# Seven half-size products for the query, key, value and gate projections of two state-space layers, and modulation sums and the rotation's swap moved off VectorE

## The reference

```python
for l in range(2):
    shift, scale, gate = split(silu(c) @ w_ada[l] + b_ada[l], 3)          # 2048 -> 3 x 2048
    h = rms_norm(x, norm_g[l]) * (1 + scale) + shift
    u, z_s, q, k, v, z_a = split(h @ w_in[l])                             # six of 1024 columns
    y_s = s5_mixer(u, ...) * silu(z_s)      # complex diagonal scan, GELU, 1024 -> 2048 GLU
    q, k = rope(q), rope(k)                 # 8 heads, two maps of 64 in each
    w = softmax(q0 k0) - lam * softmax(q1 k1)                             # causal
    y_a = rms_norm(w @ v, sub_g) * (1 - lambda_init) * silu(z_a)
    x = x + gate * (concat(y_s, y_a) @ w_out[l])                          # 2048 -> 2048
x = rms_norm(x, final_g)
x = x + gate * ((sigmoid(ga) * delta(h2) + sigmoid(gb) * window(h2)) @ w_out_2)
```

## Time and profile before

| | |
|---|---|
| Median of 3 runs | 4215.18 us (4211.24 to 4215.89) |
| Profiled execution | 4209.86 us, span of its instructions 4208.0 us |
| PE busy | 4067.2 us, 97% |
| DVE busy | 2275.8 us, 54% |
| ACT busy | 811.7 us, 19% |
| POOL busy | 496.1 us, 12% |
| Mean granted TensorE clock | 0.986 |
| HBM | 118 GB/s over the span |

### The profile page before, as it was taken

The page is one execution under the profiler, slowest core; times in us unless marked ns, Lnnn a source line. Parts: engine busy times, 40 slices in busy tenths (PEclk is TensorE's granted clock), DMA queues, the critical chain, the costliest instruction groups (busy, mean ns, idle before and its releaser), DMA issues.

```text
span 4208.0 us, 40928 instructions
## 1 busy us (share of the span) xinstructions
PE 4067.2 (97%) x15864; PEld 2733.2 (65%) x15864; DVE 2275.8 (54%) x4174; ACT 811.7 (19%) x1483; POOL 496.1 (12%) x808
## 2 busy tenths in 40 slices
PE   6999999999999999999999989999999999999999
PEld 3665544444446655444458758888888888888888
DVE  6666536664533665365656535454555347666643
ACT  2232201132012222011321222222222122320000
POOL 0233111111111332111111000000000011100000
PEclk8999999999999999999999999999999999999999
DMA  9533332334552333323345342121212243424423
GB/s 335 191 122 106 108 127 96 129 110 153 150 165 90 117 107 109 127 96 127 111 146 165 100 129 71 61 76 61 75 61 76 80 131 123 143 91 150 130 95 105
DMA packets 370127, 499.27 MB, mean 119 GB/s; under 512 B 44315, under 2 KB 279182, under 8 KB 369422
## 3 DMA queue, kind: packets, MB, share of 16 engines
q1 hardware_dynamic: 290048, 340.16, 24.9%
q0 software_dynamic: 38480, 125.86, 9.7%
q10 hardware_dynamic: 41406, 30.63, 2.3%
HBM read 462.51 MB, written 34.08 MB: 118 GB/s over the span
## 4 chain that ended last, share of the span: by engine, by line
PE 87%; DVE 8%; ACT 2%; DMA 1%; issue 1%; ACTq 0%; POOL 0%; DVEq 0%; SPq 0%; POOLq 0%
PE bank L108 85%; PE bank L111 2%; DVE tring L123 2%; DVE tring L129 2%; ACT tring L116 1%; DMA side<-in_w_ada 1%; DVE wring L123 1%; DVE dring L123 0%; DVE bank L123 0%; DVE tring L126 0%; DVE region_a L123 0%; DVE dring L126 0%; ACT L116 0%; DVE region_b L123 0%; DVE s_delta L123 0%
## 5 line engine op out<-in xcount | busy, mean ns | idle before, releaser
L108 PE MATMUL bank<-region_b,wring 128*128 128x256 f32 (+1 forms) x4416 | 1309.0, 450 | 5.0 <-ACT region_b L116 3.9
L108 PEld LDWEIGHTS bank<-region_b,wring 128*128 128x128 f32 x4416 | 829.1, 191 | 397.1 <-issue 315.8
L108 PE MATMUL bank<-region_a,wring 128*128 128x256 f32 (+1 forms) x3232 | 1067.7, 483 | 1.7 <-DVE wring L123 1.7
L108 PEld LDWEIGHTS bank<-region_a,wring 128*128 128x128 f32 x3232 | 604.7, 191 | 381.6 <-issue 335.7
L153 POOL DMA_DIRECT2D side<-in_w_ada x384 | 209.0, 545 | 1294.4 <-DVE tring L129 927.8
L129 DVE SCALAR_TENSOR_TENSOR tring<-side,cact,tring 128x512 f32<-128x512 f32 x360 | 303.0, 842 | 74.2 <-DMA side<-in_w_ada 38.4
L123 DVE TENSOR_TENSOR tring<-bank,tring 128x256 f32<-128x256 f32 (+1 forms) x229 | 101.1, 442 | 334.0 <-PE bank L108 331.0
L108 PE MATMUL bank<-wring,region_b 128*128 128x512 f32 (+1 forms) x640 | 267.5, 574 | 7.2 <-ACT region_b L116 7.2
L123 DVE TENSOR_TENSOR wring<-wring 128x1024 f32<-128x1024 f32 (+1 forms) x213 | 234.8, 1103 | 24.2 <-PE bank L108 15.2
L108 PE MATMUL bank<-wring,region_a 128*128 128x512 f32 x512 | 226.5, 600 | 4.4 <-ACT region_a L116 4.4
L108 PEld LDWEIGHTS bank<-wring,region_b 128*128 128x128 f32 x640 | 152.2, 241 | 118.2 <-issue 87.0
(11 more groups left out here) (288 smaller groups left out, 4261.5 us busy)
## 6 DMA issues: line engine op xcount, KB each, us to landing
wring<-in_w_in SPq DMA_DIRECT2D x178, 1024.0 KB, 5.3
side<-in_w_ada POOLq DMA_DIRECT2D x384, 256.0 KB, 3.1
wring<-in_w_out SPq DMA_DIRECT2D x48, 1024.0 KB, 8.0
yaT<-in_w_ada SPq DMA_DIRECT2D x16, 1024.0 KB, 9.2
wring<-in_w_glu SPq DMA_DIRECT2D x16, 1024.0 KB, 7.4
tring<-x_saved SPq DMA_DIRECT2D x48, 256.0 KB, 3.1
gring<-in_w_ada POOLq DMA_DIRECT2D x43, 256.0 KB, 3.0
SS<-in_w_ada SPq DMA_DIRECT2D x8, 1024.0 KB, 9.2
```

Of the source, the lines that this page charges most:

```text
L108: return self.e.matmul(*a, **k) if self.e else self
```

## The change

- `za`, `zs`, `q`, `k`, `v` of both layers and the first layer's output projection become seven-product jobs. `open_split` makes the quarter sums of `h`: one of them in place over `h`'s own quarter, two in `yaT`, one in `region`'s u tiles, so the last two wait for the `u` fence. The value jobs are `turned`: the weights stream in 128 columns against activations as stationary operand, 16 instead of 8 matmuls for each of the seven.
- `za` is stored in DRAM like `zs` (`save_z`) and fetched for each head in attention (`za_fetch`, SP's queue) into new places (`ya_tile`).
- Modulation sums: ACT scales the row in place, POOL adds it (`ada_sum` on both). DVE has no part in it.
- Rotation: ACT copies the four 32-partition pieces swapped from PSUM, DVE multiplies the whole tile by a sine table with changed signs.
- The next layer's parameters are cut in smaller steps, taken at 0.6 instead of 0.2 a step; the first output powers and angles move behind the next layer's norm; new tiles wait for the `out` fence.
- In the second block the quarter sums move from before the values product into its second half, and the band's rows are made earlier.
- Interleaving rates: 65 and 69 of 79 for 73 and 77, 40/37 for 45/37, opening 1.5 for 1.6.

```diff
@@ beside_states
-            yield from dense(u_job(l, 512))
+            open_split(l)
+            for n, _ in enumerate(dense(u_job(l, 512))):
+                if n == 12:
+                    for k in range(0, HT, 4):
+                        quarter(h_split[l], k, 4)
+                yield
             for h0 in range(0, HT, 2):
-                for n, _ in enumerate(dense(layer_dense(l, d["w_in"][l], 5 * HALF + h0 * P, "keep_za", h0))):
-                    if h0 == 0 and n == 3:
+                for n, _ in enumerate(gate_products(l, h0, "za", 5 * HALF)):
+                    if h0 == 0 and n == 1:
                         turn_u(l, 512)
+                        do("pe_fence", "u", l)
+                        for name in ("quarter_rest", "quarter_last"):
+                            for k in range(0, HT, 4):
+                                do(name, h_split[l], k, 4)
                     yield
...
+        def split_job(l, n0, use, *args, s3, turned_=False):
+            parts = h_split[l]
+            return Dense(d["w_in"][l], KT, n0, 256, False, None, parts.ready, use, (l, *args), parts, s3, None, turned_)
+        def gate_products(l, h0, name, n0):
+            yield from fast(split_job(l, n0 + h0 * P, "save_z", h0, name, s3=states_s3[l]),
+                            before=lambda j: temps.take(name, l, h0 + j), done=lambda j: temps.give(name, l, h0 + j))
@@ value_products
-            yield from dense(layer_dense(l, d["w_in"][l], 4 * HALF + h0 * P, "keep_v", h0, tokens="blocks", n=512))
+            for h in (h0, h0 + 2):
+                yield from fast(split_job(l, 4 * HALF + h * P, "keep_v", h, s3=lay[l]["s3_in"], turned_=True))
@@ block_one
-            interleave(state_space(l), beside, [73, 77][l] / 79)
+            do("pe_fence", "first_u", l)
+            interleave(state_space(l), beside, [65, 69][l] / 79)
-            interleave(attention(l), beside_attention(l), 45 / 37, 32, 1.6)
+            interleave(attention(l), beside_attention(l), 40 / 37, 32, 1.5)
...
-                interleave(add_gated(l, d["w_out"][l], lambda k: xT[:, k, :] if k < HT else yaT[:, k - HT, :], ready),
-                           state_space_params(1), 0.2)
+                interleave(gated, state_space_params(1), 0.6)
@@ tensor: seventh
+                        if job.turned:
+                            i = pe.matmul(bank[:, n * P:n * P + P], moving[:, n * P:n * P + P], weights[:, k, :], start=k == 0, stop=k == half - 1)
@@ vector: ada_sum removed; scalar:
+            def ada_sum(m, n0, k):
+                w = ada_slots(m).at("ada", m, n0, k)[:, 0, :]
+                act.wait_ge(*ada_landed(m, n0, k).of("ada", m, n0, k))
+                if k == 0:
+                    room(temps.clear("acc", m, n0))
+                act.activation(w if k else temps.at("acc", m, n0), w, ACT.Copy, scale=cact[:, mods[m][0] // 2, k:k + 1]).then_inc(
+                    *rows_scaled.up(m, n0, k))
@@ gpsimd
+            def ada_sum(m, n0, k):
+                if k == 0:
+                    return
+                acc = temps.at("acc", m, n0)
+                pool.wait_ge(*rows_scaled.of(m, n0, k))
+                own()
+                pool.tensor_tensor(acc, acc, ada_slots(m).at("ada", m, n0, k)[:, 0, :], AD).then_inc(*rows_added.up(m, n0, k))
+                ada_slots(m).leave(("ada", m, n0, k), pool.mine())
@@ scalar: rotate
+                for s in range(4):
+                    a, z = 32 * s, 32 * (s ^ 1)
+                    act.activation(y[z:z + 32, :], bank[a:a + 32, :], ACT.Copy).then_inc(
+                        *(att_a.up("swapped", l, h0, which, j) if s == 3 else a_step.up()))
@@ sync
+            def za_fetch(l, h):
+                sp.wait_ge(*stored("za", l, h).of("za", l, h))
+                room(passed("ssm", l) if h < HT // 2 else [valued.of(l, 3)])
+                sp.dma_start(ya_tile(l, h), za_saved[l, h]).then_inc(*za_in[h].landing(l))
@@ second block
-        for k in range(0, HT, 4):
-            quarter(h_parts, k, 4)
-            do("quarter_rest", h_parts, k, 4)
...
-        run_all(dense(vb_job))
+        values_ = dense(vb_job)
+        for n in range(6):
+            next(values_)
+        temps.take("band")
+        do("band_rows")
+        for k in range(0, HT, 4):
+            quarter(h_parts, k, 4)
+            for n in range(2):
+                next(values_)
+            do("quarter_rest", h_parts, k, 4)
+        run_all(values_)
...
+        products = gdn_products(0, 2)
+        for n in range(2):
+            next(products)
         aux.take("band")
```

More of the change, by code:

```diff
@@ L220 @@
     more: Any = None
+    turned: bool = False
     @property
@@ L494, in build, with fast @@
         jobs = []
-        def fast(job, after=None, late=()):
+        def fast(job, after=None, late=(), before=None, done=None):
             jid = len(jobs)
@@ L847, in state_space_params, with params @@
             temps.give("prow", l)
-            for part in range(2):
[L849 to L853, removed]
-                do("ssm_fetch", l, 2 + part)
[L855 to L859, removed]
+            def params(part, stages=1):
+                for stage in range(stages):
+                    do("ssm_params", l, part, stage)
+                    if l:
+                        yield
+                if not l:
+                    yield
+            for part in range(2):
+                yield from params(2 * part, 1 if part else 5)
+                yield from params(2 * part + 1, 1 if part else 5)
+                do("ssm_fetch", l, 2 + part)
+            yield from params(4, 4)
             for i in range(4):
@@ L947, in beside_attention @@
             yield from glu(l)
-        def dense_rotated(job, l, h0, which):
-            g = dense(job)
-            for j in range(2):
-                for name in ("rx", "ry"):
-                    temps.take(name, l, h0, which, j)
-            for _ in g:
-                yield
-            for j in range(2):
-                for name in ("rx", "ry"):
-                    temps.give(name, l, h0, which, j)
         def attention(l):
@@ L1498, in seventh @@
                     pe.wait_ge(*folded.of(jid, 0))
-                for k in range(half):
-                    if part < 4:
-                        room(parts.ready(half * (part // 2) + k))
-                        moving = parts.quarter(part, k)
-                    else:
-                        pe.wait_ge(*quarters_summed.of(parts.name, part - 4, parts.chunk[k]))
-                        moving = parts.sums[part - 4][:, k, :]
-                    i = pe.matmul(bank, weights[:, k, :], moving, start=k == 0, stop=k == half - 1)
+                for n in range(2 if job.turned else 1):
+                    for k in range(half):
+                        if part < 4:
+                            room(parts.ready(half * (part // 2) + k))
+                            moving = parts.quarter(part, k)
+                        else:
+                            pe.wait_ge(*quarters_summed.of(parts.name, part - 4, parts.chunk[k]))
+                            moving = parts.sums[part - 4][:, k, :]
+                        if job.turned:
+                            i = pe.matmul(bank[:, n * P:n * P + P], moving[:, n * P:n * P + P], weights[:, k, :], start=k == 0, stop=k == half - 1)
+                        else:
+                            i = pe.matmul(bank, weights[:, k, :], moving, start=k == 0, stop=k == half - 1)
                 i.then_inc(*seventh_full.up(jid, p))
@@ L2021, in quarter_last @@
                 b11, b12, _, _ = quarters_of(s, k0, n)
[L2022 removed]
+                room(s.free_last())
                 dve.wait_ge(*quarters_summed.of(s.name, 2, k0))
@@ L2244, in ssm_params @@
                     tt(cf[:, 1, :], w1[:, :], w2[:, :], SU)
+                if part == 5 and stage == 1:
                     tt(w1[:, :], a_re, a_re, M)
@@ L2258, in c_power @@
                     dve.wait_ge(*ssm_a.of("c_place", l, k - 2))
+                else:
+                    room(passed("out", l - 1))
                 def power(c):
@@ L3217, in ssm_clear @@
                 m = lay[l]
-                room(passed("att", l - 1))
+                room(passed("out", l - 1))
                 for name in ("Est", "Bst", "Cst"):
```

251 lines of the change are left out of this document (147 added, 104 removed).

## The result

The changed kernel takes 4251.43 us (median of 4 runs, 4248.63 to 4254.1) against 4213.21 us before: ratio 1.0091, 95% interval 1.0073 to 1.0108. It is 38 us slower; forecast were 84 us less. The time lies above the range.

What follows compares the result with a forecast made beforehand. The prediction took PE, busy 4067 of 4208 us, as the bound. Its terms, -132 - 21 - 15 + 48 + 6 + 20 + 6 + 4 = -84 us against 4209.86 us, gave 4126 us, range 4070 to 4188.

Steps and rivals of the forecast that it cites:

- One job on PE: Projections: a seven-product job saves 3.3 us, a turned value job 2.6 us at 25.0 us; gross gain 153 us.
- State-space rounds: Beside the scans: PE waits for sums and folds behind DVE's burst, 3 us a round, 48 us in all.
- The bound of 7 us a round: State-space rounds: upper bound of PE's wait, whole excess of burst and GpSimd's adds waited for, 112 us.
- GpSimd: Modulation adds in the rounds: 6.8 us a round on GpSimd lengthen DVE's work by 2 us.
- the forecast's third case: State-space rounds: GpSimd's adds block DVE for their whole length, 6.8 us a round, giving 4184 us; chance 0.15.
- That case's sign: Profile sign of GpSimd's adds blocking DVE for their whole length: DVE products of 1.2 us in great number.
- Modulation falls behind: Layer boundaries: 388 of 418 steps done, six sums left over, +10 us at each of two boundaries, 20 us.
- ScalarE and the fetches: ScalarE's scalings and swaps delay copies and exponentials, +6 us (0 to 25); gates' stores and refetches, 0.
- Starts: First output projection's head and small parameter instructions, 3 us each; sums before each layer's first gate job, 4 us.
- Second block: Quarter sums moved from between convolutions gain 7 us, products inside the 10.09 us hole 8; together 15 (6 to 20).
- Slower: ScalarE's in-order wait for w_ada decides once landings pass 9 us; 4241 us at 0.3 us per sum; chance 0.05.
- case 1: State-space rounds near break-even, PE waiting 3 us a round: 4126 us, own range 4100 to 4152; chance 0.47.

Runs made afterwards that it cites:

- Experiment 4: The changed kernel with GpSimd's modulation add on one column instead of 512, scalings and waits kept: 4164.69 us, ratio 0.9884.
- experiment 8: The changed kernel with plain gates in the rounds and a faster modulation pace, modulation sums still on ScalarE and GpSimd: 4149.25 us, ratio 0.9852.
- 7: The changed kernel with plain gates in the rounds, modulation sums back on VectorE and pace 1.25, 1.85, 2.0: 4126.88 us, ratio 0.98.
- experiment 2: The changed kernel with 1.3, 1.9 and 2.0 modulation steps per projection step for 1.25, 1.7 and 1.8: 4216.15 us, ratio 1.0011.
- experiment 11: Plain gates, sums on VectorE and faster pace, with the gates' fetches of heads 4 to 7 asked for later: 4124.16 us, ratio 0.9791.
- experiment 3: The changed kernel with the two gates beside the state-space rounds as plain jobs again: 4153.12 us, ratio 0.9859.

## Why the prediction was wrong, point by point

**One job on PE: right.** 3.3 us a job; the seventh of a turned value job, 32 records, is 3.57 us from one to the next,

```profile
642.63 3.74 PE L108 MATMUL bank<-s_in,region_a 128*128 128x128 f32 x32
646.20 3.74 PE L108 MATMUL bank<-wring,region_b 128*128 128x128 f32 x32
```

so 25.0 us for seven, as worked out.

**State-space rounds: the step that failed**, "PE waits 0 to 3.4 us, 1.5 on the mean; with GpSimd's 2 us, 3 us". The mechanism, PE waiting for a fold or sum behind DVE's burst, is what the traces show for 30.3 of the 39.4 idle us in layer 0 and 22.5 of 41.4 in layer 1; its size was not 3 us. PE is idle 5.6 us a round of layer 0 (39.5/7). Over that, the same products take longer: 277.0/7 = 39.6 us of busy PE instead of 36.3, as the clock falls after the holes. The forecast looked at the clock only to see that none was to be gained, and priced a hole by its own length. It also laid only sums and folds against the burst, and not ScalarE's copies behind the sines, which ended 19.0 us in layer 1. Rounds of 39.3 us were expected and 45.2 measured; in layer 1, by the same working from 42.1, 41.8 and 46.4. Over the seven rounds from scan to scan that is 74 us, and taken for all eight 8 x 5.9 + 8 x 4.6 = 84 us, of the 125 us of error. The bound of 7 us a round did not contain it: the rounds are 8.9 and 7.6 us above the unhindered 36.3 and 38.8. Experiment 4 splits the error. Without GpSimd's adds the rounds are still 5.9 and 5.5 us above, where 1.5 was taken; the adds then cost 3.1 and 2.1 us, where another 1.5 was taken. So the larger miss is the wait behind the burst with its slow clock, and not GpSimd.

**GpSimd: mechanism right, DVE's share near, the rest of the kernel left out.** DVE is busy 33.9 us a round of layer 0, forecast 33, and 31.5 in experiment 4, so the adds lengthen its instructions by 2.5 us a round where 2 was taken. Outside the rounds nothing was taken, and the move costs 22 us there with plain gates (experiment 8 against 7). DVE's weight sums went from 1.22 to 1.48 us on the mean. The Trainium skill's rule (SBUF — State Buffer, "Who interferes with whom") is that of a DVE instruction with two SBUF inputs and a GpSimd instruction that reads SBUF one blocks the other for a whole instruction. The rotation product of 0.69 us at 2.13 us beside an add of 1.28 us agrees with it. As a price for a round it is only an upper bound: 6.8 us by the forecast's third case, 2.5 measured. That case's sign, 128x320 products of 1.2 us in great number, did not come: 30 of 96 are above 1.1 us, 24 before. Its 4184 us was still too low.

**Modulation falls behind: right in mechanism, mis-sized.** The count of 388 against 418 steps holds; seven sums were left, not six. The holes grew by 17.9 and 18.1 us, not 10 each. At the first the last sum ends 16.0 us behind the last product, where 11 had been worked out: seven adds follow each other at 2.15 us from one to the next, 1.27 of add and 0.55 of issuing the next row's DMA, and ScalarE waits 1.3 to 3.5 us for each of four refetched rows. Together 35 us (experiment 2) for 20.

**Attention and output projections.** Together from last scan to last product the layers gained 35 and 24 us where 54 and 34 were forecast. Nearly all that is missing is in the output projections. From last scan to their first product the time fell by 28.5 and 34.3 us, where 34 each was forecast. The projections themselves changed by -6 and +11 us where -20 and 0 were forecast. Experiment 4, without GpSimd's adds, has them at 203.6 and 196.8 us, for 222.8 and 196.6 before: -19 and 0. So the term that failed here is GpSimd's, which was put at nothing outside the rounds. ScalarE and the fetches, +6 and 0 us in the sum, were the smaller matter. The stored gates were ready early, but their places weren't: the fetch of head 4 needs the place of head 3's values, and SP's queue stood before it with two weight loads behind, 12 us of waits, of which taking them away gave back 3 (experiment 11). The prediction had looked at the data's due time and not at the place's.

**Starts.** Second block: 13 us alone, forecast 15. Starts of the layers: 3 us, forecast 4 for the sums before the first gate job. First output projection: 226 to 219 us where 206 was forecast; its head is 1.2 + 3.8 us of waiting for 3, a small part of the difference.

**The chances.** Slower had 0.05, by a wait on ScalarE for w_ada. ScalarE does wait for these rows, but experiment 4 keeps its scalings and waits and is 87 us faster, and experiment 3 keeps them and is 98 us faster. The real cause was case 1's own mechanism at nearly three times the size, 8.9 us a round with the slow clock for 3. The danger of the change, one instruction of slack on an engine at 91%, was named. But the range's upper end of 4188 us is only what the bound of 7 us a round gives by itself (16 x 4 = 64 us more, 4190), with nothing left for the other terms.

## What to carry to other kernels

A scheme that gives PE less work but makes its steps wait for instructions of another engine should be laid against the longest burst in that engine's queue: here it paid in attention and, once GpSimd's adds were gone, in the first output projection, and it cost 49 us beside the scans. Look for a second way from the busy queue to PE as well, here ScalarE's copies behind the sines. Price a hole in PE with the slow clock behind it, and a job with fewer steps with everything else that is paced by steps. Work moved to GpSimd isn't free for VectorE; look at the length of VectorE's instructions after such a move, not at its busy share.

## What was not expected of the hardware

After holes of 2.9 to 7.9 us in a full PE the granted clock fell to 1.2 GHz, seven times in the seven rounds of layer 0, and not after the one of 2.0 us: sixteen 256-column records took 5.6 us instead of 3.45 at 351.79 us. Rounds with such holes had a mean clock of 0.93, with plain gates 1.00. GpSimd's 128x512 adds took 1.36 us on average, and beside them DVE's 128x1024 sums 1.48 us instead of 1.24; taking 5 us of DVE's work a round in exchange for 5 such adds left DVE busy 1.3 us less and made PE wait longer.
